# Feature chunks with 512-column matmuls, a shared last row block and folded key weights in a two-layer decoder trunk

## The chip, the cores and the metric

One NeuronCore of a Trainium2 chip runs the whole program. The metric is the device time of one execution in microseconds. A core has TensorE (PE; its weight loads are shown apart as PEld), VectorE (DVE), ScalarE (ACT), GpSimd (POOL), and SyncE (SP), whose queue issues the DMA transfers here.

## What is computed

Two layers of a decoder trunk over 256 tokens of width 2048. Cut to what matters:

```python
(r_q, r_k, r_v, a_cq, a_ckv, a_kpe, l_x, l_v, l_o, l_i, l_f, c_q, z) = _split_cols(x @ w_in, IN_SPLITS)
ret  = _merge(_head_norm(_retention(r_q, r_k, r_v, positions), ret_norm_g))
mla  = _merge(_mla(a_cq, a_ckv, a_kpe, ...))
xc   = jax.nn.silu(_causal_conv(l_x, ml_conv_w, ml_conv_b))
lq   = jnp.einsum('bshd,hde->bhse', xc_h, ml_w_q)      # 4 heads, 128x128 weights each
lk   = jnp.einsum('bshd,hde->bhse', xc_h, ml_w_k)
cell = _mlstm(lq, lk, lv, i_pre, f_pre) * jax.nn.sigmoid(l_o)
mls  = _merge(_head_norm(cell, ml_norm_g)) + ml_skip * xc
memo = _merge(_mem_attention(c_q, mem, w_mem_kv))      # 256 memory tokens
y    = jnp.concatenate([ret, mla, mls, memo], -1) * jax.nn.silu(z)
x    = _layernorm(DEEPNORM_ALPHA * x + y @ w_out, ln_g, ln_b)
```

In `_mlstm` the keys enter only through the scores of queries and keys. All data are fp32; weights are read from HBM once.

## The kernel before, in words

**Chunks and slots.** The weights of a layer are a stream of 20 chunks (`CHUNKS`): memk, memv, lx, cq, akv, aq, lv, lo, rq, rk, rv, z3, z2, z1, z0, out0 to out4. Most are 512 columns wide. Each has 16 slots, one for each block of 128 rows of its weight, so a layer has 320 slots. SP loads two slots at a time into `raw`, four pairs deep; the DMA of pair m waits until the remainder of slot 2m - 7 is done.

**High and low parts.** A product of fp32 numbers is made of three fp32r matmuls. ScalarE writes the high part of each slot (`hi`, L839), VectorE the remainder (`lo`, L1192), both in rings of five (`RING`). x (and the memory and y) are held as high and low parts too: xh, xl, mh, ml. ScalarE's hi of slot t waits until TensorE has used slot t - 5, so it runs at most five slots ahead.

**The two layouts.** In a "tok" chunk x is the weights operand and `hi` streams through: per slot 2 x (xh hi, xl hi), then 2 x (xh lo), six matmuls of 512 columns (L1125, L1126, L1129). In a "feat" chunk (memk, lx, cq, z3 to z0) the result is wanted with features on the partitions, so `hi` is the weights operand and x streams through: for four blocks j of 128 features a matmul with xh (L1135) and one with xl (L1137), 256 columns each, adding into the same half of a PSUM bank; then four with `lo` (L1141). Two accumulators of two banks are used in turn. TensorE may begin a chunk once the chunk before the last has been read.

**Other work** is put between slots by tables written out by hand: `PE_AT`, `ACT_AT`, `DVE_AT` give for a slot position the steps that an engine does after its own part of that slot, in order. Each engine has one queue, so a step that waits holds up all that stands behind it. TensorE's small products go through four more PSUM banks in turn. Those that matter here:
- memk and cq are split into high and low parts: ScalarE at 20, 22 and 68, 69, VectorE's remainders (L1277) at 21, 23 and 69, 70. `mem_scores` (L866 to L868) of head 0 stands on TensorE after slot 69 and waits for all of them. memv's copies and remainders are VectorE's at 36, 38.
- lx is copied (L696), run through a convolution on VectorE (positions 54 to 61), then silu on ScalarE at 65, 66. `ml_q` and `ml_k` (L922, fp32 matmuls, 256 columns, two instructions each) stand at 88 to 91, their copies on ScalarE at 93 to 95, the scores L964 and L965 from 110.
- x is split (`x_hi`, `x_lo`), with one x block of two per two slots, VectorE at 16 to 30 in layer 0 and at 21 to 35 in layer 1.
- `silu` of z reads the accumulator, `gate` multiplies, then y is split (`y_hi`, `y_lo`) before the out chunks.

**The end.** The last chunk of layer 1 stays resident, and TensorE does all 16 slots for rows 0 to 127 first, then for rows 128 to 255 (L1157 to L1161). VectorE does `residual(3)`, then for each row block of 128: last residual, statistics, X - mean times gain (L1618), GpSimd's power, times 1/std plus bias (L1624). Block 0 is done in 1024 columns, block 1 in 512; each piece is then stored by SP (L587). The code of VectorE's last part:

```python
for n in range(0, D_MODEL + ahead * w, w):
    if n < D_MODEL:
        blk = X[:, i, n:n + w]
        link(dve.scalar_tensor_tensor(blk, blk, ln_mv[:, i, 0:1], gb[:, 0, n:n + w],
                                      ALU.subtract, ALU.mult))
    if n >= ahead * w:
        ...
        dve.wait_ge(ln_pow.sem, ln_pow.at(l, i))
        dve.scalar_tensor_tensor(blk, blk, ln_rstd[:, i:i + 1], gb[:, 1, at], ALU.mult, ALU.add)\
           .then_inc(finished.sem, 1)
```

`link` makes VectorE wait for its own operation.

## Time and profile before

| | |
|---|---|
| median of 3 runs | 935.68 us (935.43 to 936.45) |
| profiled execution, its own time | 935.72 us |
| its span, first to last instruction | 933.9 us |
| TensorE busy | 919.6 us (98%) |
| VectorE busy | 631.9 us (68%) |
| ScalarE busy | 492.2 us (53%) |
| granted TensorE clock, mean | 0.995 |
| HBM | 184 GB/s over the span |

### The profile page before, as it was taken

To read this page: it belongs to the slowest core of one execution; us is meant where nothing else is said; L and a number is where in the kernel's file an instruction comes from. 1 tells how busy PE (TensorE), PEld (TensorE's weight loads), DVE (VectorE), ACT (ScalarE), POOL (GpSimd) and SP (SyncE) were. 2 spreads that over 40 slices of the span, in tenths; PEclk is the share of its full clock that TensorE was granted. 3 is DMA by queue.
4 is the path that set the end of the run, shared out by engine and by line. 5 is a ranking of instruction groups with operands and counts; after the bars stand their busy time and mean duration, and the time that the engine had idled before them with its cause. 6 is when DMAs were issued, how large, how long until landed. Compare 5 with 4: busy or idle time off the path is not lost.

```text
span 933.9 us, 15656 instructions
## 1 busy us (share of the span) xinstructions
PE 919.6 (98%) x5876; PEld 836.5 (90%) x5876; DVE 631.9 (68%) x1264; ACT 492.2 (53%) x925; POOL 16.0 (2%) x18
## 2 busy tenths in 40 slices
PE   8999999999999999999999999999999999999994
PEld 7899998888889999888998999888888999998894
DVE  6867677766754765665759577767577557767657
ACT  5654765544554444544576456745354544555441
POOL 0000000000000000000000000000000000000001
PEclk9999999999999999999999999999999999999998
DMA  9874546655444555663765765466355554565843
GB/s 345 307 275 161 158 137 201 212 166 178 138 159 158 169 171 180 186 195 115 249 195 191 253 210 173 142 202 180 114 156 148 171 159 151 180 186 175 289 135 126
DMA packets 51868, 172.67 MB, mean 185 GB/s; under 512 B 6216, under 2 KB 6352, under 8 KB 51152
## 3 DMA queue, kind: packets, MB, share of 16 engines
q1 hardware_dynamic: 51792, 171.66, 57.5%
q8 instruction: 47, 0.77, 0.3%
q14 instruction: 29, 0.24, 0.1%
HBM read 169.53 MB, written 2.11 MB: 184 GB/s over the span
## 4 chain that ended last, share of the span: by engine, by line
PE 95%; DVE 2%; DMA 2%; issue 0%; ACT 0%; SPq 0%; DVEq 0%; ACTq 0%
PE acc L1125 17%; PE acc L1129 17%; PE acc L1126 17%; PE acc L1135 11%; PE acc L1141 11%; PE acc L1137 11%; PE work L861 2%; DMA raw<-in_w 2%; PE work L1004 1%; PE work L922 1%; PE work L964 1%; PE work L866 1%; PE work L867 1%; PE work L868 1%; DVE X L1618 1%; PE work L1039 1%
## 5 line engine op out<-in xcount | busy, mean ns | idle before, releaser
L1192 DVE TENSOR_TENSOR lo<-raw,hi 128x512 fp32r<-128x512 f32 (+2 forms) x624 | 394.5, 646 | 278.5 <-ACT hi L839 270.9
L839 ACT ACTIVATE hi<-raw 128x512 fp32r<-128x512 f32 (+2 forms) x624 | 365.4, 595 | 348.3 <-PE acc L1129 175.2
L1125 PE MATMUL acc<-hi,xh 128*128 128x512 f32 (+2 forms) x592 | 219.3, 375 | 0.0
L1126 PE MATMUL acc<-hi,xl 128*128 128x512 f32 (+2 forms) x592 | 211.3, 362 | 0.0
L1135 PE MATMUL acc<-xh,hi 128*128 128x256 f32 x768 | 194.1, 285 | 0.0
L1137 PE MATMUL acc<-xl,hi 128*128 128x256 f32 x768 | 192.4, 283 | 0.0
L1129 PE MATMUL acc<-lo,xh 128*128 128x512 f32 (+2 forms) x592 | 166.1, 362 | 0.0
L1137 PEld LDWEIGHTS acc<-xl,hi 128*128 128x128 f32 x768 | 146.9, 191 | 0.2
L1135 PEld LDWEIGHTS acc<-xh,hi 128*128 128x128 f32 x768 | 146.8, 191 | 0.2
L1126 PEld LDWEIGHTS acc<-hi,xl 128*128 128x128 f32 x592 | 111.7, 189 | 15.0
L1125 PEld LDWEIGHTS acc<-hi,xh 128*128 128x128 f32 x592 | 111.6, 188 | 15.0
L1141 PE MATMUL acc<-xh,lo 128*128 128x256 f32 x768 | 123.4, 283 | 0.0
L1129 PEld LDWEIGHTS acc<-lo,xh 128*128 128x128 f32 x592 | 106.3, 188 | 17.1
L1141 PEld LDWEIGHTS acc<-xh,lo 128*128 128x128 f32 x768 | 105.9, 191 | 0.0
L1135 PE MATMUL acc<-mh,hi 128*128 128x256 f32 x128 | 33.0, 290 | 0.3 <-ACT hi L839 0.3
L1137 PE MATMUL acc<-ml,hi 128*128 128x256 f32 x128 | 32.6, 286 | 0.0
L1135 PEld LDWEIGHTS acc<-mh,hi 128*128 128x128 f32 x128 | 24.8, 194 | 1.5 <-issue 1.5
L1125 PE MATMUL acc<-hi,mh 128*128 128x512 f32 x64 | 25.8, 402 | 0.0
L1126 PE MATMUL acc<-hi,ml 128*128 128x512 f32 x64 | 25.0, 391 | 0.0
L1137 PEld LDWEIGHTS acc<-ml,hi 128*128 128x128 f32 x128 | 24.8, 194 | 0.1
L1141 PE MATMUL acc<-mh,lo 128*128 128x256 f32 x128 | 20.6, 283 | 0.0
L1129 PE MATMUL acc<-lo,mh 128*128 128x512 f32 x64 | 19.8, 390 | 0.0
(294 smaller groups left out, 1024.6 us busy)
## 6 DMA issues: line engine op xcount, KB each, us to landing
raw<-in_w SPq DMA_DIRECT2D x255, 512.0 KB, 3.7
raw<-in_w SPq DMA_DIRECT2D x50, 256.0 KB, 2.7
raw<-in_w SPq DMA_DIRECT2D x16, 328.0 KB, 3.2
Y<-in_wuq SPq DMA_DIRECT2D x2, 1152.0 KB, 7.8
Y<-in_x_t SPq DMA_DIRECT2D x4, 512.0 KB, 8.5
X<-in_x SPq DMA_DIRECT2D x4, 512.0 KB, 4.6
gb<-in_gb SPq DMA_DIRECT2D x1, 2048.0 KB, 7.3
Y<-in_gb SPq DMA_DIRECT2D x1, 2048.0 KB, 10.3
```

The lines of the kernel that those rows point to most:

```text
L839: act.activation(place(l, t, hi), raw[:, s, (t % 2) * w:(t % 2 + 1) * w], ACT.Copy)\
L861: return pe.transpose(dst, src, ident[0:src.shape[0], 0:src.shape[0]])
L866: pe.matmul(o, ah, bh, start=start, stop=False)
L867: pe.matmul(o, al, bh, start=False, stop=False)
L868: return pe.matmul(o, ah, bl, start=False, stop=stop)
L1125: pe.matmul(o, ah[:, kk, q], hi[:, s, 0:w], start=k == 0, stop=False)
L1126: pe.matmul(o, al[:, kk, q], hi[:, s, 0:w], start=False, stop=False)
L1129: m = pe.matmul(acc[:, p, i, 0:w], ah[:, kk, i * P:(i + 1) * P], lo[:, s, 0:w], start=False, stop=k == KT - 1)
L1135: pe.matmul(o, hi[:, s, q], ah[:, kk, :], start=k == 0 and j % 2 == 0, stop=False, skip_group_check=True)
L1137: pe.matmul(o, hi[:, s, q], al[:, kk, :], start=False, stop=False, skip_group_check=True)
L1141: m = pe.matmul(o, lo[:, s, q], ah[:, kk, :], start=False, stop=k == KT - 1, skip_group_check=True)
L1192: dve.tensor_tensor(place(*at, lo), raw[:, s, (t % 2) * w:(t % 2 + 1) * w], place(*at, hi).bitcast(F32), ALU.subtract).then_inc(lo_done.se ...
```

## The change

Three edits are made together.

1. Feature chunks are cut in halves of 256 features (`_halves`), each of 8 slots; a slot then holds two blocks of 128 rows, side by side. xh and xl lie interleaved in one buffer `xx` (mh and ml in `mm`), so that one matmul of 512 columns multiplies a block of `hi` by both; high sums lie in columns 0 to 255 of a bank and low sums in 256 to 511. ScalarE copies the low sums to SBUF (`part`), VectorE adds the high sums (`joined`) and gives the accumulator back. silu, and the splits of memk and cq, then read SBUF. memv comes ahead of memk. The number of slots stays at 320; silu, gate and split positions move.
2. In the matrix memory, Wq and Wk of a head are multiplied once (`ml_fold`, four fp32 matmuls of 128 columns, after slot 64; ScalarE's copy at 67), `ml_q` multiplies xc by that product, and the scores take xc itself as keys. `ml_k` and its copies go; `skip`, which overwrites xc, moves from 101 to 126.
3. In the last row block, VectorE does the four subtractions in a row without waiting for itself, and the final step of two of the four pieces only. For the other two TensorE adds the bias (identity times bias) and diag(1/std) times the piece in PSUM, and ScalarE copies the result. `residual(3)` of layer 1 moves from behind the stream into it, at slots 314 and 317.

```diff
-CHUNKS = [("memk", W, "feat"), ("memv", W, "tok"), ("lx", W, "feat"), ("cq", W, "feat"),
+FEAT = W // 2
+
+
+def _halves(*names):
+    return [(f"{n}{q}", FEAT, "feat") for n in names for q in range(2)]
+
+
+CHUNKS = [("memv", W, "tok"), *_halves("memk", "lx", "cq"),
           ("akv", AKV_W, "tok"), ("aq", QRANK - QHEAD, "tok"), ("lv", W, "tok"), ("lo", W, "tok"),
-          ("rq", W, "tok"), ("rk", W, "tok"), ("rv", W, "tok"),
-          ("z3", W, "feat"), ("z2", W, "feat"), ("z1", W, "feat"), ("z0", W, "feat"),
+          ("rq", W, "tok"), ("rk", W, "tok"), ("rv", W, "tok"), *_halves("z3_", "z2_", "z1_", "z0_"),
...
+SPAN = [KT // 2 if layout == "feat" else KT for _, _, layout in CHUNKS]
+WIDTH = [2 * w if layout == "feat" else w for _, w, layout in CHUNKS]
+SLOT_AT = np.concatenate([[0], np.cumsum(SPAN)]).tolist()
+PLACE = [(c, k) for c in range(NCH) for k in range(SPAN[c])]
...
-        (88, "ml_q", 0), (88, "ml_q", 1), (89, "ml_k", 0), (91, "ml_k", 1),
+        (64, "ml_fold", 0), (88, "ml_q", 0), (89, "ml_q", 1),
...
-        (20, "memk", 0), (22, "memk", 1), (52, "lx", 0), (53, "lx", 1),
-        (65, "silu_conv", 0), (66, "silu_conv", 1), (68, "cq", 0), (69, "cq", 1), (84, "akv", 0), (85, "akv", 1),
-        (93, "ml_q", 0), (94, "ml_q", 1), (95, "ml_k", 0), (95, "ml_k", 1),
+        (28, "part", "memk", 0), (36, "part", "memk", 1), (44, "part", "lx", 0), (52, "part", "lx", 1),
+        (60, "part", "cq", 0), (68, "part", "cq", 1),
+        (188, "part", "z3_", 0), (196, "part", "z3_", 1), (204, "part", "z2_", 0), (212, "part", "z2_", 1),
+        (220, "part", "z1_", 0), (228, "part", "z1_", 1), (236, "part", "z0_", 0), (244, "part", "z0_", 1),
+        (30, "memk", 0), (38, "memk", 1),
+        (65, "silu_conv", 0), (66, "silu_conv", 1), (62, "cq", 0), (70, "cq", 1), (84, "akv", 0), (85, "akv", 1),
+        (67, "ml_fold", 0), (93, "ml_q", 0), (94, "ml_q", 1),
...
-        (36, "memv", 0), (38, "memv", 1), (99, "mem_out", 0), (110, "mem_out", 1),
+        (20, "memv", 0), (22, "memv", 1),
+        (29, "joined", "memk", 0), (37, "joined", "memk", 1), (45, "joined", "lx", 0), (53, "joined", "lx", 1),
+        (61, "joined", "cq", 0), (69, "joined", "cq", 1),
+        (189, "joined", "z3_", 0), (197, "joined", "z3_", 1), (205, "joined", "z2_", 0), (213, "joined", "z2_", 1),
+        (221, "joined", "z1_", 0), (229, "joined", "z1_", 1), (237, "joined", "z0_", 0), (245, "joined", "z0_", 1),
+        (99, "mem_out", 0), (110, "mem_out", 1),
         (123, "lo", "wukv", 0), (125, "lo", "wukv", 1), (128, "lo", "ckvT", 0),
-        (21, "lo", "memk", 0), (23, "lo", "memk", 1), (69, "lo", "cq", 0), (70, "lo", "cq", 1),
+        (31, "lo", "memk", 0), (39, "lo", "memk", 1), (63, "lo", "cq", 0), (71, "lo", "cq", 1),
...
-        _put(DVE_AT, (OUT0 + _c + 1) * KT + 4, "residual", _c)
+        _put(DVE_AT, SLOT_AT[OUT0 + _c + 1] + 4, "residual", _c)
     else:
-        _put(FIRST_DVE, (OUT0 + _c + 1) * KT + 4, "residual", _c)
+        _put(FIRST_DVE, SLOT_AT[OUT0 + _c + 1] + 4, "residual", _c)
+        _put(LATER_DVE, SLOT_AT[OUT0 + _c + 1] + 4 + 6, "residual", _c, 0)
+        _put(LATER_DVE, SLOT_AT[OUT0 + _c + 1] + 4 + 9, "residual", _c, 1)
...
+        xx = sb("xx", [P, KT, 2, SEQ], F32R)
+        xh, xl = xx[:, :, 0, :], xx[:, :, 1, :]
...
+        qk = B[3][:, 0:512].rearrange("p (h d) -> p h d", h=HEADS)
...
+                if i == 0:
+                    sp.wait_ge(finished.sem, b + 1)
+                elif b < 2 + BY_MATMUL:
+                    sp.wait_ge(copied.sem, b - 2 + 1)
+                else:
+                    sp.wait_ge(finished.sem, b - BY_MATMUL + 1)
...
+                def part_(name, q):
+
+                    c = CI[f"{name}{q}"]
+                    wait_chunk(act, l, c)
+                    if (name, q) == ("z3_", 0):
+                        wait_read(act, l, ("ml_scores", 3))
+                    if (name, q) == ("z2_", 0):
+                        wait_job(act, l, ("rkT", 1))
+                    if (name, q) == ("z0_", 0):
+                        wait_job(act, l, ("retT", 1))
+                    act.activation(sums(name, q), acc[:, acc_turn(l, c)[1], :, SEQ:2 * SEQ], ACT.Copy)\
+                       .then_inc(lo_part.sem, 1)
...
+                def ml_fold(_):
+                    wait_job(act, l, ("ml_fold", 0))
+                    act.wait_ge(conv_done.sem, conv_done.at(l, 0))
+                    act.activation(qk[:, :, :], bank(l, ("ml_fold", 0)).rearrange("p (h d) -> p h d", h=HEADS), ACT.Copy)\
+                       .then_inc(free_bank(l, "ml_fold", 0), 1)
...
+                    wait_joined(act, l, f"z{g}_", i)
+                    act.activation(sums(f"z{g}_", i), sums(f"z{g}_", i), ACT.Silu).then_inc(silu_done.sem, 1)
...
+            l = DEPTH - 1
+            act.wait_ge(ln_pow.sem, ln_pow.at(l, 1))
+            act.activation(tmp[:, 0:P], ident, ACT.Copy, scale=ln_rstd[:, 1:2]).then_inc(diag_done.sem, 1)
+            for b in range(BY_MATMUL):
+                act.wait_ge(scaled.sem, b + 1)
+                act.activation(X[:, 1, b * 512:(b + 1) * 512], A_out3(b), ACT.Copy).then_inc(copied.sem, 1)
...
-                        wait_acc_read(pe, l, CI["memk"])
-                        wait_acc_read(pe, l, CI["cq"])
+                        pe.wait_ge(kq_split.sem, kq_split.at(l, 3))
...
+                def ml_fold(_):
+
+                    pe.wait_ge(lw_in.sem, lw_in.at(l, 0))
+                    o = take("ml_fold", 0)
+                    for h in range(HEADS):
+                        m = pe.matmul(o[:, h * HD:(h + 1) * HD], lw[:, 0, h, :], lw[:, 1, h, :], start=True, stop=True)
+                    m.then_inc(job_done.sem, 1)
...
+                def ml_q(q):
+                    if q == 0:
+                        wait_read(pe, l, ("ml_fold", 0))
+                    pe.wait_ge(xc_done.sem, xc_done.at(l, q))
+                    o = take("ml_q", q)
+                    for h in (2 * q, 2 * q + 1):
+                        m = pe.matmul(o[:, (h % 2) * 256:(h % 2 + 1) * 256], qk[:, h, :], xcT[:, h, :],
+                                      start=True, stop=True)
...
-                    causal_scores(take("ml_scores", h), lkT, lqT, h).then_inc(job_done.sem, 1)
+                        wait_read(pe, l, ("ml_q", 0), ("ml_q", 1))
+                    causal_scores(take("ml_scores", h), xcT, lqT, h).then_inc(job_done.sem, 1)
...
-                        for j in range(4):
-                            o, q = acc[:, p, j // 2, (j % 2) * 256:(j % 2 + 1) * 256], slice(j * P, (j + 1) * P)
-                            pe.matmul(o, hi[:, s, q], ah[:, kk, :], start=k == 0 and j % 2 == 0, stop=False,
-                                      skip_group_check=True)
-                            pe.matmul(o, hi[:, s, q], al[:, kk, :], start=False, stop=False, skip_group_check=True)
+                        for kk in range(2):
+                            x = both_parts[:, 2 * k + kk, :, :].rearrange("p a t -> p (a t)")
+                            for j in range(2):
+                                q = slice(kk * FEAT + j * P, kk * FEAT + (j + 1) * P)
+                                pe.matmul(acc[:, p, j, :], hi[:, s, q], x, start=k == 0 and kk == 0, stop=False,
+                                          skip_group_check=True)
                         pe.wait_ge(lo_done.sem, lo_done.at(l, t))
-                        for j in range(4):
-                            o, q = acc[:, p, j // 2, (j % 2) * 256:(j % 2 + 1) * 256], slice(j * P, (j + 1) * P)
-                            m = pe.matmul(o, lo[:, s, q], ah[:, kk, :], start=False, stop=k == KT - 1,
-                                          skip_group_check=True)
+                        for kk in range(2):
+                            for j in range(2):
+                                q = slice(kk * FEAT + j * P, kk * FEAT + (j + 1) * P)
+                                m = pe.matmul(acc[:, p, j, 0:SEQ], lo[:, s, q], both_parts[:, 2 * k + kk, 0, :], start=False,
+                                              stop=2 * k + kk == KT - 1, skip_group_check=True)
...
+            wait_acc_read(pe, l, LAST - 1)
+            pe.wait_ge(gb_in.sem, 16)
+            for b in range(BY_MATMUL):
+                pe.matmul(A_out3(b), ident, gb[:, 1, b * 512:(b + 1) * 512], start=True, stop=False)
+            pe.wait_ge(diag_done.sem, 1)
+            for b in range(BY_MATMUL):
+                pe.wait_ge(gained.sem, b + 1)
+                pe.matmul(A_out3(b), tmp[:, 0:P], X[:, 1, b * 512:(b + 1) * 512], start=False, stop=True)\
+                  .then_inc(scaled.sem, 1)
...
+                def joined_(name, q):
+
+                    p = acc_turn(l, CI[f"{name}{q}"])[1]
+                    dve.wait_ge(lo_part.sem, lo_part.at(l, JOINED.index((name, q))))
+                    dve.tensor_tensor(sums(name, q), acc[:, p, :, 0:SEQ], sums(name, q), ALU.add).then_inc(joined.sem, 1)
+                    wait_joined(dve, l, name, q)
+                    dve.sem_inc(acc_read[p].sem, 2)
...
-            link(residual(c - 1))
...
-                ahead = 2 * 512 // w
-                for n in range(0, D_MODEL + ahead * w, w):
-                    if n < D_MODEL:
-                        blk = X[:, i, n:n + w]
-                        link(dve.scalar_tensor_tensor(blk, blk, ln_mv[:, i, 0:1], gb[:, 0, n:n + w],
-                                                      ALU.subtract, ALU.mult))
-                    if n >= ahead * w:
-                        at = slice(n - ahead * w, n - ahead * w + w)
-                        blk = X[:, i, at]
-                        dve.wait_ge(ln_pow.sem, ln_pow.at(l, i))
-                        dve.scalar_tensor_tensor(blk, blk, ln_rstd[:, i:i + 1], gb[:, 1, at], ALU.mult, ALU.add)\
-                           .then_inc(finished.sem, 1)
+                for n in range(0, D_MODEL, w):
+                    blk = X[:, i, n:n + w]
+                    m = dve.scalar_tensor_tensor(blk, blk, ln_mv[:, i, 0:1], gb[:, 0, n:n + w], ALU.subtract, ALU.mult)
+                    m.then_inc(gained.sem, 1) if i else link(m)
+                if i:
+                    dve.wait_ge(gained.sem, D_MODEL // w)
+                dve.wait_ge(ln_pow.sem, ln_pow.at(l, i))
+                for n in range(BY_MATMUL * w if i else 0, D_MODEL, w):
+                    blk = X[:, i, n:n + w]
+                    dve.scalar_tensor_tensor(blk, blk, ln_rstd[:, i:i + 1], gb[:, 1, n:n + w], ALU.mult, ALU.add)\
+                       .then_inc(finished.sem, 1)
...
-        "lw": np.stack([np.stack([g["ml_w_q"][l], g["ml_w_k"][l]]).transpose(2, 0, 1, 3).reshape(-1) for l in range(DEPTH)]),
+        "lw": np.stack([np.stack([g["ml_w_q"][l], g["ml_w_k"][l]]).transpose(3, 0, 1, 2).reshape(-1) for l in range(DEPTH)]),
```

The rest of the diff follows from these: names and indices of accumulators, buffers for the sums, the order of the weights in HBM.

## Rows read from the trace of the kernel before

**Rows 1.** The page's part 1: busy us (share of the span), instructions.
```profile
PE 919.6 (98%) x5876; PEld 836.5 (90%) x5876; DVE 631.9 (68%) x1264; ACT 492.2 (53%) x925; POOL 16.0 (2%) x18
```

**Rows 2.** Who waited: engine, line waited for, us in total, times, longest.
```profile
ACT hi L839 <- PE acc L1129: 175.2, 261, 2.6
ACT hi L839 <- PE acc L1141: 155.2, 195, 2.2
...
PE acc L1135 <- ACT hi L839: 0.3, 1, 0.3
```

**Rows 3.** Timeline of TensorE in cq: start us, duration us, engine, line.
```profile
89.03 0.28 PE L1135 MATMUL acc<-xh,hi 128*128 128x256 f32 x1
...
90.47 0.28 PE L1135 MATMUL acc<-xh,hi 128*128 128x256 f32 x1
```

**Rows 4.** Timeline of TensorE in a token chunk, lv.
```profile
140.27 0.39 PE L1125 MATMUL acc<-hi,xh 128*128 128x512 f32 x1
...
141.63 0.39 PE L1125 MATMUL acc<-hi,xh 128*128 128x512 f32 x1
```

**Rows 5.** Timeline of TensorE in out0 of layer 1.
```profile
836.09 0.39 PE L1125 MATMUL acc<-hi,B2r 128*128 128x512 f32 x1
...
837.49 0.39 PE L1125 MATMUL acc<-hi,B3r 128*128 128x512 f32 x1
```

**Rows 6.** Groups by form: busy us, mean ns, idle before.
```profile
L1192 DVE TENSOR_TENSOR lo<-raw,hi 128x512 fp32r<-128x512 f32 x512 | 347.5, 690 | 239.9 <-ACT hi L839 232.8 <-PE acc L1129 3.2
...
L839 ACT ACTIVATE hi<-raw 128x512 fp32r<-128x512 f32 x512 | 318.6, 630 | 316.8 <-PE acc L1129 153.3 <-PE acc L1141 149.7 <-DMA raw<-in_w 12.7
...
L696 ACT ACTIVATE B<-acc 128x512 f32<-128x512 f32 x4 | 2.3, 582 | 0.0
```

**Rows 7.** Busy us of PE, PEld, DVE, ACT, POOL in two stretches of layer 1.
```profile
497.00:510.00 13.00, 13.00 (x67) 10.71 (x66) 12.53 (x23) 8.89 (x17) 0.00 (x0) 1.00 0.61 199
510.00:523.00 13.00, 13.00 (x107) 12.87 (x106) 9.89 (x16) 6.19 (x11) 0.00 (x0) 1.00 0.64 205
```

**Rows 8.** The chain in order of time, one piece.
```profile
121.10 1.73 PE work L922 x8
```

**Rows 9.** Timelines of the three engines around mem_scores(0), layer 0.
```profile
97.93 0.42 ACT L839 ACTIVATE hi<-raw 128x256 fp32r<-128x256 f32 x1 [0.33 <-PE acc L1141]
98.25 0.58 ACT L691 ACTIVATE B2r<-acc 128x512 fp32r<-128x512 f32 x1
98.73 0.41 ACT L839 ACTIVATE hi<-raw 128x256 fp32r<-128x256 f32 x1
...
99.51 0.69 DVE L1277 TENSOR_TENSOR B5r<-acc,B2r 128x512 fp32r<-128x512 f32 x1
100.11 0.42 DVE L1192 TENSOR_TENSOR lo<-raw,hi 128x256 fp32r<-128x256 f32 x1
100.45 0.69 DVE L1277 TENSOR_TENSOR B5r<-acc,B2r 128x512 fp32r<-128x512 f32 x1
...
97.67 0.28 PE L1125 MATMUL acc<-hi,xh 128*128 128x256 f32 x1
...
101.99 0.29 PE L866 MATMUL work<-B0r,B2r 128*128 128x256 f32 x1
```

**Rows 10.** Timelines of the tail, three engines.
```profile
915.31 0.39 PE L1157 MATMUL acc<-ml,xh 128*128 128x256 f32 x1
...
925.35 2.32 DVE L1618 SCALAR_TENSOR_TENSOR X<-X,ln_mv,Y 128x512 f32<-128x512 f32 x3
...
929.15 2.08 DVE L1624 SCALAR_TENSOR_TENSOR X<-X,ln_rstd,Y 128x512 f32<-128x512 f32 x3
...
925.51 0.99 POOL L597 TENSOR_TENSOR ln_rstd<-ln_stats,half 128x1 f32<-128x1 f32 x1 [4.99 <-DVE ln_stats L1612]
```

**Rows 11.** Busy time, granted clock (PEclk), DMA share, GB/s at the end.
```profile
922.00:923.00 1.00, 0.15 (x2) 0.00 (x0) 1.00 (x2) 0.00 (x0) 0.00 (x0) 1.00 0.00 0
925.00:926.00 1.00, 0.00 (x0) 0.00 (x0) 0.90 (x3) 0.00 (x0) 0.49 (x1) 0.59 0.99 406
```

224 lines of the change are left out of this document (113 added, 111 removed).

## The prediction

> **What bounds the kernel now.** I read the page's engine row first: TensorE is busy 98% of 933.9 us [rows 1]. The list of who waited for whom then says that TensorE hardly waits (0.3 us for weights once the work has begun), while ScalarE stands 175.2 + 155.2 us waiting for TensorE to give ring buffers back [rows 2]. So TensorE's queue sets the time from about 5 us to 922 us and whatever is taken from it is gained, as long as ScalarE and VectorE keep their lead, which is the ring's five slots. Behind 922 us a tail on VectorE and the stores decides (part 5). So three things are to be costed: the matmul rate of feature chunks, places where a shorter lead or a new dependency stops TensorE, and the tail.
>
> **Part 1, merged matmuls.** Two feature slots start 90.47 - 89.03 = 1.44 us apart; with 12 matmuls of 256 columns that is 0.12 us each [rows 3]. Two token slots start 141.63 - 140.27 = 1.36 us apart, 0.2267 us for each of six matmuls of 512 columns [rows 4]. The 256 columns between them take 0.1067 us, which is 2.4 GHz; the other 0.0133 us comes once for each matmul, whatever its width. The change streams the same columns in 4 matmuls of 512 and 4 of 256: 4 x 0.2267 + 4 x 0.12 = 1.387 us, 0.053 us less. Seven chunks of 16 slots in two layers are 224 slots: 11.9 us.
>
> No row has a 512-column matmul with hi as its weights. The nearest other one, with B buffers as weights in out0, takes 837.49 - 836.09 = 1.40 us for six, a fixed part of 0.020 us [rows 5]: 224 x 4 x 0.0067 = 6 us less gain. I allow as much below. I take 0.0133, which these weights (hi) and this moving operand (xh) show now.
>
> The Trainium skill (TensorE: Matmul & The Clock Gate, section Back-to-back issue gap) gives a warm start-to-start of N/2.4 + 2.5 ns, 109 and 216 ns, which speaks against this part: by it 896 vanished matmuls save 2.2 us only. This trace disagrees (120 and 227 ns).
>
> **Its price.** High and low sums now stand side by side, so each of 14 half chunks per layer costs ScalarE a copy (128x512 from PSUM, 0.58 us) and VectorE an addition (0.69 us) [rows 6]. That is 28 x 0.69 = 19 us and 28 x 0.58 = 16 us, the latter less lx's four copies. In a feature slot of 1.387 us the stream itself takes 0.63 and 0.69 us [rows 6], so both are covered by about 0.7 us of idle per slot. An accumulator is needed back 8 slots after its half chunk ends and is added up at the fifth or sixth position after it, by engines that run up to five slots ahead: no wait. Cost 0; with the lead gone, each addition would cost up to 0.69 us.
>
> The lead is thinnest where x is split. In layer 1 from 497 to 510 us VectorE is busy 12.53 of 13.00 us, and 9.89 in the next 13 [rows 7]. There the change puts memv's four operations (2.7 us, in place of memk's two, 1.3) and, by position 39, two additions and memk's two remainders (2.6 us): 4 us more, against a lead that I estimate at 4 to 5 us (five slots of 1.44 less the stream's own 1.3 and what the split takes). I take 0; bounds 0 and 2 us per layer.
>
> **Part 2, folded key weights.** Eight instructions of L922 (256 columns; an fp32 matmul is two instructions) run in 1.73 us, 0.216 each, and each layer has 16 [rows 8]. The change leaves 8 and adds a fold of four matmuls of 128 columns, 8 instructions. I estimate those at half of 0.216: 0.87 us. Saved 2 x (1.73 - 0.87) = 1.7 us; bounds 1.3 (fixed parts as in part 1) and 2.0.
>
> **Part 3, where the fold and the halves land.** The fold stands after slot 64, ScalarE's copy of it at position 67. ScalarE reaches 67 while TensorE is at slot 63, so it stops there, in order, until the fold is through. Behind it are queued hi(68), the part copy of cq1, hi(69), hi(70), the high part of cq1 and hi(71); VectorE's addition (69) and remainder (71) of cq1 wait for them, and TensorE wants that last remainder for mem_scores(0) after slot 69. Before, the second cq remainder (B5r) ran 100.45 to 101.14 and mem_scores started at 101.99: a margin of 0.85 us [rows 9].
>
> With time 0 at the start of slot 64 (97.67 before) and the spacings of rows 9 (hi 0.32, copy 0.48, lo 0.34, remainder 0.60, next slot's start to the reader 0.26):
> - the fold ends at 0.72 + 0.87 = 1.59, its copy starts at 1.85;
> - hi(68) 2.33, part 2.65, hi(69) 3.13 to 3.55;
> - VectorE lo(69) 3.59, addition 3.93 to 4.62;
> - high part of cq1 4.67, hi(71) 5.17 to 5.59;
> - lo(71) 5.62, remainder of cq1 5.96 to 6.65; TensorE may go at 6.7.
>
> TensorE is there at 1.59 + 5 x 0.72 = 5.19. So it stands 1.5 us in each layer: +3.0 us. Bounds 0 (the margin swallows it) and 2.5 us each.
>
> **Part 4, the start.** memv comes first, a token chunk of 1.36 instead of 1.44 us per slot. The first two slots lie ahead of TensorE's only wait for weights, so 2 x 0.08 us is not gained: +0.2.
>
> **Part 5, the tail.** Of row block 1 VectorE now does four subtractions and two final operations, TensorE two blocks. VectorE's last eight operations run from 925.35 to 931.23 [rows 10]. After: start 925.5 (below), six at 0.69 with no wait between the four, done 929.7, 1.5 us earlier. TensorE: the power takes 0.99 us [rows 10], so it is ready at 926.65; diagonal by ScalarE, about 0.3, 927.0; product 4 x 0.216 = 0.86, copy 0.58: block 0 at 928.8, block 1 at 929.6. But four stores leave through SP in the order b2, b3, b4, b5. Now 2.67 us lie between VectorE's last operation and the end; 262 KB at 406 GB/s [rows 11] are 0.65 us of that, and I put 1.0 ahead of the flow and 1.0 behind it. One after another: b3 flows from 930.6, b4, b5 until 932.6, the end 933.65 instead of 933.9: -0.25 us. Most of what VectorE saves goes to the stores. Bounds -1.5 and +1.
>
> Moving residual(3) into slots 314 and 317 frees VectorE earlier, but puts 0.8 us twice between remainders for which TensorE already waits (a start is late at 915.31 [rows 10]). TensorE's first half ends 0.9 us later, VectorE starts block 0 0.1 us later; that is in the numbers above.
>
> **Sum** against the profiled execution's own 935.72 (span 933.9 and 1.8 around it; the median of the runs, 935.68, is the same within 0.04): 935.7 - 11.9 - 1.7 + 3.0 + 0.2 - 0.25 = **925.1 us**.
>
> **Rivals.**
> - *The keys' wait does not come*, the margin of rows 9 absorbs it: 922.1. For it: TensorE never waits now. Against: the order of the positions. Chance 0.14.
> - *The clock falls before the products.* It fell at about 925.2, 3.0 us after the last matmul [rows 11]. Now TensorE works on the bias blocks until 924.8 and resumes at 927.1, a gap of 2.3 us. If it falls, two products take 1.72 us each, b3 is ready at 931.3, SP holds b4 and b5 behind it, the end is near 934.8: 926.3. Chance 0.16.
> - *VectorE's lead runs out while x is split*: 1 to 4 us, 927.5. Chance 0.12.
> - *A merged matmul costs 0.233* as in rows 5: 931.1. Chance 0.04.
> - *A merge saves hardly anything*, 2.2 us in place of 11.9 (what the page cited above would give): 934.8, no change. Rows 3 and 4 speak against it. Chance 0.04.
> - *Slower: accumulators come back late.* With each half chunk's addition exposed (28 x 0.69), 925.1 + 19 = 944. It decides from 10.6 / 28 = 0.38 us per half chunk. Against it: 0.7 us of idle per slot. Chance 0.03.
>
> My forecast has 0.47. The range 921 to 929 holds it and the first three rivals, 0.89 together, less their edges. About 0.2% (1.9 us) is what a measurement of this kernel can tell from no change. Faster by more: 0.93; within it 0.04; slower by more 0.03.
>
> **What would show it.** Part 1: a z slot starts every 1.387 us. Part 2: 8 fold instructions in 0.87 us after slot 64. Part 3: TensorE idle for about 1.5 us ahead of mem_scores(0) in each layer, released by VectorE's remainder of cq. Part 5: granted clock 1.0 in the products, stores back to back. The prediction is wrong if z slots stay at 1.44, if TensorE has no such gap, or if waits for lo appear between slots 20 and 40.

## The result and the profile after

The changed kernel takes **929.53 us** (median of 4 runs, 929.0 to 929.95), the kernel before 935.96 beside it. The ratio is 0.9928, 95% interval 0.9916 to 0.9940: faster by 6.4 us where 10.6 were forecast, and 0.5 us above the range. The profiled execution took 929.15 us, its span is 927.4 us.

The page's part 1 of the kernel after, answering to [rows 1]:

```profile
PE 912.3 (98%) x4988; PEld 788.5 (85%) x4988; DVE 646.6 (70%) x1290; ACT 502.9 (54%) x950; POOL 16.0 (2%) x18
```

TensorE has 888 matmuls fewer, and VectorE and ScalarE are 14.7 and 10.7 us busier, as the change says. The list of who waited for whom (us in total, times, longest), answering to [rows 2]:

```profile
ACT hi L906 <- PE acc L1212: 162.3, 222, 2.6
...
ACT hi L906 <- PE acc L1226: 131.2, 192, 2.1
...
PE work L941 <- DVE B5r L1371: 2.7, 2, 1.4
PE acc L1257 <- ACT tmp L914: 2.3, 1, 2.3
...
PE acc L1208 <- ACT hi L906: 1.8, 1, 1.8
PE acc L1247 <- DVE mm L1288: 0.9, 2, 0.5
```

ScalarE still waits for ring buffers, 293 us where it was 330, so TensorE still sets the time. TensorE's new waits are the keys' (L941, two times), the one for the diagonal in the tail (L1257), a longer one at the start (L1208; 0.3 before), and two for remainders in the first half of the last tile (L1247), where `residual(3)` now stands between them. There is none for lo while x is split.

**Feature slots.** Timeline of TensorE in cq of layer 0, answering to [rows 3] (start, duration, engine, line; x4 is four matmuls in a row):

```profile
89.75 1.09 PE L1220 MATMUL acc<-xx,hi 128*128 128x512 f32 x4
90.68 0.63 PE L1226 MATMUL acc<-xx,lo 128*128 128x256 f32 x4
91.15 1.09 PE L1220 MATMUL acc<-xx,hi 128*128 128x512 f32 x4
92.08 0.64 PE L1226 MATMUL acc<-xx,lo 128*128 128x256 f32 x4
92.56 1.09 PE L1220 MATMUL acc<-xx,hi 128*128 128x512 f32 x4
...
93.96 1.09 PE L1220 MATMUL acc<-xx,hi 128*128 128x512 f32 x4
```

Three slots take 93.96 - 89.75 = 4.21 us, 1.403 each, not 1.387. The four wide matmuls (512 columns) take 0.93 us instead of 4 x 0.2267 = 0.91; the four narrow ones (256 columns) 0.47 to 0.48, as they should.

**The keys.** Timelines of the three engines from slot 64 to `mem_scores(0)` in layer 0, answering to [rows 9]:

```profile
97.48 1.05 PE L994 MATMUL work<-B 128*128 128x128 f32 x8
98.29 0.36 PE L1208 MATMUL acc<-hi,xx 128*128 128x256 f32 x1
...
98.57 0.60 ACT L831 ACTIVATE B<-work 128x512 f32<-128x512 f32 x1 [1.70 <-PE work L994]
...
99.37 0.59 ACT L767 ACTIVATE B<-acc 128x512 f32<-128x512 f32 x1
...
101.35 0.63 ACT L754 ACTIVATE B2r<-B 128x512 fp32r<-128x512 f32 x1 [0.79 <-DVE B L1647]
...
100.64 0.68 DVE L1647 TENSOR_TENSOR B<-acc,B 128x512 f32<-128x512 f32 x1
...
102.67 0.68 DVE L1371 TENSOR_TENSOR B5r<-B,B2r 128x512 fp32r<-128x512 f32 x1
...
103.50 0.35 PE L941 MATMUL work<-B0r,B2r 128*128 128x256 f32 x1 [1.37 <-DVE B5r L1371]
```

One link after the other: ScalarE stood 1.70 us for the fold, the part copy (L767) came after it, then VectorE's addition (L1647), the high part (L754), the remainder (L1371), and TensorE, idle for 1.37 us.

**The tail.** Timelines of TensorE, VectorE and ScalarE at the end of the kernel after, answering to [rows 10]:

```profile
916.34 1.88 PE L1253 MATMUL acc<-Y,ident 128*128 128x512 f32 x4
920.48 1.98 PE L1257 MATMUL acc<-X,tmp 128*128 128x512 f32 x4 [2.26 <-ACT tmp L914]
...
917.42 0.42 DVE L1708 SCALAR_TENSOR_TENSOR X<-X,acc 128x256 f32<-128x256 f32 x1
...
918.84 2.73 DVE L1717 SCALAR_TENSOR_TENSOR X<-X,ln_mv,Y 128x512 f32<-128x512 f32 x4
921.60 1.42 DVE L1724 SCALAR_TENSOR_TENSOR X<-X,ln_rstd,Y 128x512 f32<-128x512 f32 x2
...
922.50 0.60 ACT L917 ACTIVATE X<-acc 128x512 f32<-128x512 f32 x1 [0.26 <-PE acc L1257]
```

The products (L1257, four instructions) ran at the full clock, 1.98 us in all. VectorE does the four subtractions in a row (L1717) and two final operations (L1724). It ends at 923.0, ScalarE at 923.1, yet the program goes on to 927.4. The same stretch in windows (busy time of PE, PEld, DVE, ACT, POOL, then granted clock, DMA share, GB/s):

```profile
923.00:924.00 1.00, 0.00 (x0) 0.00 (x0) 0.01 (x1) 0.10 (x1) 0.00 (x0) 1.00 0.75 277
924.00:925.00 1.00, 0.00 (x0) 0.00 (x0) 0.00 (x0) 0.00 (x0) 0.00 (x0) 1.00 1.01 373
925.00:926.00 1.00, 0.00 (x0) 0.00 (x0) 0.00 (x0) 0.00 (x0) 0.00 (x0) 1.00 1.05 354
```

With no engine at work, the last four blocks (1.05 MB) drain until a little past 926.

### The profile page after: what moved, and what is told of

It reads as the page before. It is cut to its first block, busy times and chain, and to the rows that moved or that the text cites. A ratio compares the mean times of both kernels' runs of the same rounds, so it can differ in the third digit from the quotient of the medians.

```text
span 927.4 us, 13974 instructions
## 1 busy us (share of the span) xinstructions
PE 912.3 (98%) x4988; PEld 788.5 (85%) x4988; DVE 646.6 (70%) x1290; ACT 502.9 (54%) x950; POOL 16.0 (2%) x18
## 4 chain that ended last, share of the span: by engine, by line
PE 95%; DMA 1%; DVE 1%; issue 1%; ACT 1%; POOL 0%; SPq 0%; POOLq 0%; DVEq 0%
PE acc L1220 22%; PE acc L1208 17%; PE acc L1212 17%; PE acc L1209 17%; PE acc L1226 11%; PE work L936 2%; DMA raw<-in_w 1%; PE work L1084 1%; PE work L1044 1%; PE work L941 1%; PE work L942 1%; PE work L943 1%; PE work L1119 1%; PE work L1120 1%; PE work L1069 1%
## 5 line engine op out<-in xcount | busy, mean ns | idle before, releaser
L1208 PE MATMUL acc<-hi,xx 128*128 128x512 f32 (+2 forms) x592 | 219.4, 375 | 0.0
L1209 PE MATMUL acc<-hi,xx 128*128 128x512 f32 (+2 forms) x592 | 211.2, 361 | 0.0
L1220 PE MATMUL acc<-xx,hi 128*128 128x512 f32 x768 | 211.1, 396 | 0.0
L1212 PE MATMUL acc<-lo,xx 128*128 128x512 f32 (+2 forms) x592 | 166.1, 362 | 0.0
L1220 PEld LDWEIGHTS acc<-xx,hi 128*128 128x128 f32 x768 | 131.3, 189 | 17.6
L1226 PEld LDWEIGHTS acc<-xx,lo 128*128 128x128 f32 x768 | 117.7, 189 | 16.4
L1209 PEld LDWEIGHTS acc<-hi,xx 128*128 128x128 f32 x592 | 111.7, 189 | 14.9
L1208 PEld LDWEIGHTS acc<-hi,xx 128*128 128x128 f32 x592 | 111.6, 188 | 14.9
L1226 PE MATMUL acc<-xx,lo 128*128 128x256 f32 x768 | 122.0, 281 | 0.0
L1212 PEld LDWEIGHTS acc<-lo,xx 128*128 128x128 f32 x592 | 106.2, 188 | 16.9
L1220 PE MATMUL acc<-mm,hi 128*128 128x512 f32 x128 | 35.5, 399 | 0.0
L1208 PE MATMUL acc<-hi,mm 128*128 128x512 f32 x64 | 25.5, 399 | 1.8 <-ACT hi L906 1.8
L1209 PE MATMUL acc<-hi,mm 128*128 128x512 f32 x64 | 24.9, 389 | 0.0
L1208 PEld LDWEIGHTS acc<-hi,mm 128*128 128x128 f32 x64 | 12.1, 189 | 5.3 <-DVE mm L1293 2.2
```

Of the source, the lines that this page charges most:

```text
L1208: pe.matmul(o, ah[:, q], hi[:, s, 0:w], start=k == 0, stop=False)
L1209: pe.matmul(o, al[:, q], hi[:, s, 0:w], start=False, stop=False)
L1212: m = pe.matmul(acc[:, p, i, 0:w], ah[:, i * P:(i + 1) * P], lo[:, s, 0:w], start=False, stop=k == KT - 1)
L1220: pe.matmul(acc[:, p, j, :], hi[:, s, q], x, start=k == 0 and kk == 0, stop=False, skip_group_check=True)
L1226: m = pe.matmul(acc[:, p, j, 0:SEQ], lo[:, s, q], both_parts[:, 2 * k + kk, 0, :], start=False, stop=2 * k + kk == KT - 1, skip_group_chec ...
```

## The experiments

Differences are against the changed kernel unless another is named; times are medians of several executions, but of a single one for the kernels of "Layout, order, place", "All eight matmuls wide" and "Ring slots shifted". Of diffs the deciding lines are shown; "..." marks what is left out. The kernel before ran beside each batch (935.8 to 936.3).

### Where the merge's gain went

**The merge alone undone.** hi meets the high and the low x in two matmuls into the same bank.

```diff
-    pe.matmul(acc[:, p, j, :], hi[:, s, q], x, ...)
+    pe.matmul(acc[:, p, j, 0:SEQ], hi[:, s, q], x[:, 0:SEQ], ...)
+    pe.matmul(acc[:, p, j, SEQ:2 * SEQ], hi[:, s, q], x[:, SEQ:2 * SEQ], ...)
```

> The changed kernel with the merge alone undone: in a feature chunk hi still meets the high and the low x, but in two matmuls of 256 columns into the two halves of the same accumulator, 12 matmuls a slot. Order, layout, additions, fold and tail stay. Theory: each matmul costs 0.12 us as before, a slot 1.44 us, so 224 slots take 224 x (1.44 - 1.4035) = 8.2 us more than the changed kernel: 937.7, which is slower than the kernel before by the additions' side effects, the keys' wait and the tail. Rival (a merge saves only 2.5 ns for each matmul that is gone, and the shorter slot has another cause such as the layout of x): slot near 1.41 us, 2.2 us more: 931.7.

937.88 us; every feature slot without other work takes 1.44. Timeline of TensorE in cq:

```profile
89.79 0.28 PE L1220 MATMUL acc<-xx,hi 128*128 128x256 f32 x1
...
91.23 0.28 PE L1220 MATMUL acc<-xx,hi 128*128 128x256 f32 x1
```

91.23 - 89.79 = 1.44 us, 0.12 for each of twelve. So the merge is worth 937.88 - 929.53 = 8.35 us, 0.037 us per slot, and the other parts together cost 1.7 us against the kernel before that ran beside it (936.19; ratio 1.0017, 1.0008 to 1.0027). The ten executions of this kernel lie between 936.3 and 938.8, so TensorE's own way says it more firmly. Its first matmul of the last tile, in the kernel before, the changed one and this one:

```profile
909.59 0.28 PE L1157 MATMUL acc<-ml,B1r 128*128 128x256 f32 x1
902.73 0.28 PE L1243 MATMUL acc<-mm,B1r 128*128 128x256 f32 x1
911.02 0.28 PE L1245 MATMUL acc<-mm,B1r 128*128 128x256 f32 x1
```

911.02 - 902.73 = 8.3 us is the merge, 911.02 - 909.59 = 1.4 us all the rest ahead of the last tile.

**Layout, order, place.** Three kernels ask what makes a merged matmul dearer than the 0.2267 us of a token slot. In the first, high and low x are in separate halves of the buffer:

```diff
-        xx = sb("xx", [P, KT, 2, SEQ], F32R)
+        xx = sb("xx", [P, 2, KT, SEQ], F32R)
...
```

> The changed kernel with the high and the low x in two separate halves of their buffer, so that a merged matmul of 512 columns reads two runs of 256 columns 2,048 elements or more apart instead of one run of 512. Theory A (the larger fixed part, 0.233 us for each merged matmul, comes from something else, such as which buffer holds the weights): feature slots stay at 1.40 us, 929 in all. Theory B (it comes from how the moving operand is laid out): feature slots move by more than 0.01 us, to 1.387 if this layout is the better one (925.5) or above 1.41 if it is worse (over 931).

929.25 us, slots unchanged: 1.403. (Here the granted clock fell within the products at the end, 0.73 from 920 to 921 us and 0.50 behind, which made the tail 1.0 us longer; more on this under "The tail".) Next, the two loops exchanged:

```diff
-    for kk in range(2):
-        x = both_parts[:, 2 * k + kk, :, :]...
-        for j in range(2):
+    for j in range(2):
+        for kk in range(2):
+            x = both_parts[:, 2 * k + kk, :, :]...
```

> The changed kernel with the loops of a feature slot exchanged: both inner pieces (kk) of one half (j) behind each other, so that the accumulator buffers of two matmuls that follow each other are 0,0,1,1 as in token slots, and the moving operand changes with each matmul. Theory (a merged matmul's 0.233 us comes from changing the accumulator bank, or from two matmuls with one moving operand): slot 1.36 to 1.39 us, 2 to 9 us less than the changed kernel's 929.5. Rival (it comes from the weights' side): slot stays at 1.40, time at 929.5.

928.75 us, slots 1.403. And the rings placed first in SBUF:

```diff
+        hi, lo = sb("hi", [P, RING, 512], F32R), sb("lo", [P, RING, 512], F32R)
         X = sb("X", [P, NT, D_MODEL])
...
-        hi, lo = sb("hi", [P, RING, 512], F32R), sb("lo", [P, RING, 512], F32R)
```

> The changed kernel with the rings of hi and lo weights placed in front of all other buffers of SBUF instead of behind them; no instruction changes otherwise. Theory: the fixed part of a matmul depends on where the weights lie beside the moving operand (512 columns take 0.227 us where a ring buffer moves and xx is the weights, 0.233 where a later buffer is the weights); then the feature slots fall to 1.36 to 1.387 us and the token slots may rise from 1.36 to 1.40 us. With 224 feature slots and 400 token slots: anywhere from 926 to 941. Rival (the place in SBUF plays no part): 1.40 and 1.36 us stay, 929.5 in all.

928.36 us, feature slots 1.403, token slots 1.36. Of each of the three there is one execution, 0.3 to 1.2 us below the changed kernel's median, and feature slots have no part in that: in the traces the mean distance from one matmul of a feature slot to the next moved by less than 1 ns at each of its eight places. Neither the moving operand's layout nor the order of banks nor which buffer lies first is the cause.

**All eight matmuls wide.**

```diff
-    m = pe.matmul(acc[:, p, j, 0:SEQ], lo[:, s, q], both_parts[:, 2 * k + kk, 0, :], ...)
+    m = pe.matmul(acc[:, p, j, :], lo[:, s, q], <both halves, 512 columns>, ...)
```

> The changed kernel with lo too meeting the high and the low x in one matmul of 512 columns: it adds the product of the two low parts, which neither kernel computes, so a feature slot has eight matmuls of 512 columns and no narrow one. What sets the time of a merged matmul? Theory A (the mixture of 512 and 256 columns within a slot costs it): all eight take 0.2267 us, slot 1.813 us. Theory B (hi or lo as weights with x moving cost 0.233 whatever stands beside them): slot 1.87 us. 224 slots longer by 0.41 or 0.46 us: 1,021 or 1,033 us in all; the slot is what counts here.

1,022.77 us. Timeline of TensorE in cq:

```profile
99.83 1.07 PE L1220 MATMUL acc<-xx,hi 128*128 128x512 f32 x4
...
103.45 1.07 PE L1220 MATMUL acc<-xx,hi 128*128 128x512 f32 x4
```

(103.45 - 99.83) / 16 = 0.226 us per matmul, with the same hi, x, banks and places. Theory A holds: a merged matmul costs what a token matmul costs as long as no narrow one stands in the slot.

**Feature slots in pairs.** The wide matmuls of two slots, then the narrow ones of both; the base also has the fold moved and the B buffers placed alike (both below).

```diff
+    for u in () if k % 2 == 0 else (t - 1, t):
+        pe.wait_ge(lo_done.sem, lo_done.at(l, u))
+        ... the four lo matmuls of slot u ...
```

> The kernel with all B buffers placed alike (expected at 924.8), and feature slots taken in pairs: the hi matmuls of two slots (eight of 512 columns), then the lo matmuls of both (eight of 256). Same matmuls, half as many changes of width. A pair takes 2.807 us now; 2.773 is what it would be with 227 and 120 ns each. Theory A (each change of width costs, or disturbs the matmuls for a while): the pair falls by half of the difference or more, 0.017 to 0.034 us x 112 pairs = 1.9 to 3.8 us less: 921.0 to 922.9. Theory B (narrow and wide matmuls in one slot cost the same however they are ordered): pair stays at 2.80, 924.8. Rival on the other side: ring buffers come free one slot later, ScalarE's lead of 4.7 us shrinks and TensorE starts to wait for hi or lo: over 925.

924.89 us. Timeline of TensorE: the first pair of memk, which comes behind a token chunk, then a pair of cq:

```profile
29.45 1.98 PE L1221 MATMUL acc<-mm,hi 128*128 128x512 f32 x8
31.26 1.12 PE L1229 MATMUL acc<-mm,lo 128*128 128x256 f32 x8
...
90.88 2.00 PE L1221 MATMUL acc<-xx,hi 128*128 128x512 f32 x8
92.72 1.11 PE L1229 MATMUL acc<-xx,lo 128*128 128x256 f32 x8
93.67 1.09 PE L1221 MATMUL acc<-xx,hi 128*128 128x512 f32 x4
```

Behind wide matmuls, eight wide ones take 31.26 - 29.45 = 1.81 us, 0.2267 each. Behind narrow ones the same eight take 92.72 - 90.88 = 1.84 us. Going from narrow to wide costs about 0.03 us, and a pair has one such change: 2.79 us where two slots took 2.81. In the trace the five wide matmuls behind a change start 0.228 to 0.236 us apart, the next ones 0.227.

The mechanism is theory A's, the size is not. A pair fell by 0.014 us and not by 0.017 or more: the change is felt over five wide matmuls, a slot has only four of them and is 0.016 us dearer than 1.387, a pair has all five and is 0.020 dearer than 2.773. And the time missed theory A's 921.0 to 922.9. It is 0.3 us below its base, but TensorE reached the last tile at 898.90 us and in the base at 898.42; that it is no slower comes from the tail, where the base's clock fell in the profiled execution and this one's did not (below). The wait for cq grew (1.2 us in all instead of 0.5).

### Where the weights lie

**Ring slots shifted.** The rings' rows are made 520 elements long.

```diff
-        hi, lo = sb("hi", [P, RING, 512], F32R), sb("lo", [P, RING, 512], F32R)
+        hi, lo = sb("hi", [P, RING, 520], F32R), sb("lo", [P, RING, 520], F32R)
```

> The changed kernel with ring slots 2,080 instead of 2,048 bytes apart, so that each of the five slots starts at another offset (0, 32, 64, 96 and 128 bytes); the buffers allocated behind the rings move by 320 bytes. Theory: if the fixed part depends on how the addresses of weights and moving operand stand to each other, slot times spread with a period of five slots, by 0.01 us or more. Rival: address plays no part; every feature slot stays at 1.40 to 1.406, the first 8 slots of out0 at 1.40 and the others at 1.36; 929.5 in all.

934.30 us, 4.8 more. The slots of cq repeat with a period of five, 1.415, 1.405, 1.401, 1.416, 1.396 us, where they were 1.401 and 1.406 in turn: the theory's spread. Timeline of TensorE in the second half of out0, where xx holds the weights:

```profile
387.24 0.39 PE L1208 MATMUL acc<-hi,xx 128*128 128x512 f32 x1
...
388.64 0.39 PE L1208 MATMUL acc<-hi,xx 128*128 128x512 f32 x1
...
390.01 0.40 PE L1208 MATMUL acc<-hi,xx 128*128 128x512 f32 x1
...
391.40 0.39 PE L1208 MATMUL acc<-hi,xx 128*128 128x512 f32 x1
```

1.40, 1.37 and 1.39 us where all were 1.36. So the place of an operand does count, in steps much finer than which buffer comes first.

**B buffers at multiples of 128 bytes.** From here to the end of this section the base is the kernel with the fold moved (next section, 926.41). X, xx, mm, hi and lo all start 128 bytes past a multiple of 2,048; B1 to B3 start 1,984 past one and B0 1,952. The edit moves these four.

```diff
+        sb("gap", [P, 24])
...
-            size = {0: NT * HEADS * (HD + 1), 3: 4 * (SEQ + PAD)}.get(i, 4 * SEQ)
+            size = {0: NT * HEADS * (HD + 1) + 24, 3: 4 * (SEQ + PAD) + 16}.get(i, 4 * SEQ)
```

> The kernel with the fold moved behind the keys (926.4), and with gaps of 96, 96 and 64 bytes in SBUF so that the B buffers start at multiples of 128 bytes, as xx, mm and the rings do. Before, B1 to B3 start 64 bytes and B0 32 bytes off such a multiple; they hold the weights of the first 8 slots of each out chunk. Theory (a 512-column matmul takes 0.233 instead of 0.227 us where an operand isn't aligned to 128 bytes, as the shifted ring made token slots slower): these slots fall from 1.40 to 1.36 us, 0.71 to 0.68 in the half-wide ones; 6 x 8 x 0.04 = 1.9 us less, and 0.4 to 1 for out3 and out4: 923.8 to 924.5. Rival (alignment isn't what slows them): 1.40 stays, 926.4.

925.31 us, 1.1 less than its base. Timeline of TensorE in out0 of layer 1 (weights B1, B2, B3, then B0):

```profile
823.91 0.39 PE L1209 MATMUL acc<-hi,B1r 128*128 128x512 f32 x1
...
825.27 0.39 PE L1209 MATMUL acc<-hi,B2r 128*128 128x512 f32 x1
...
832.11 0.40 PE L1209 MATMUL acc<-hi,B0r 128*128 128x512 f32 x1
...
833.51 0.40 PE L1209 MATMUL acc<-hi,xx 128*128 128x512 f32 x1
```

825.27 - 823.91 = 1.36 us with B1, 833.51 - 832.11 = 1.40 with B0, which now stood at a multiple of 2,048, 128 bytes off the others. The theory was half right: two of eight slots stayed slow, and the time missed its 923.8 to 924.5. The 256-wide slots of out3 and out4 got slower, from 0.71 to 0.72, which takes back 0.2 us.

**All placed alike.**

```diff
+        stats, rstd = sb("stats", [P, 8, 6]), sb("rstd", [P, 8])      # moved here, fills 224 bytes
         B, Br = [], []
...
-            size = {0: NT * HEADS * (HD + 1), 3: 4 * (SEQ + PAD)}.get(i, 4 * SEQ)
+            size = {0: NT * HEADS * (HD + 1) + 56, 3: 4 * (SEQ + PAD) + 20}.get(i, 4 * SEQ)
```

> The kernel with the fold moved behind the keys (926.4), with B0 to B3 all placed at 128 bytes past a multiple of 256, as xx, mm and the rings are (buffers of statistics and gaps fill the space). With B0 at a multiple of 256 and B1 to B3 as here, only six of the first eight slots of an out chunk had fallen to 1.36 us (925.3); those with B0 stayed at 1.40. Theory (what counts is that weights and moving operand stand alike to a multiple of 256 bytes): all eight take 1.36, six chunks x 2 x 0.04 = 0.5 us less than with six: 924.8. Rival (B0's slots are slow for another reason): 1.40 stays there, 925.3.

925.20 us. All eight early slots take 1.36 us, now with B0 too (timeline of out0 in layer 1):

```profile
829.79 0.39 PE L1209 MATMUL acc<-hi,B0r 128*128 128x512 f32 x1
...
831.15 0.39 PE L1209 MATMUL acc<-hi,B0r 128*128 128x512 f32 x1
```

With weights and moving operand alike to 256 bytes every wide matmul behind wide ones takes 0.2267 us, and where they are not, up to 0.236. The fixed 0.020 us of [rows 5] was this and had nothing to do with hi or x. TensorE reached the last tile 1.2 us earlier than in the kernel with six fast slots (0.3 of it from the start), and yet the time is the same; the tail took it back (below).

### The keys' wait

```diff
-        (64, "ml_fold", 0), ...      # TensorE
+        (76, "ml_fold", 0), ...
-        (67, "ml_fold", 0), ...      # ScalarE's copy
+        (82, "ml_fold", 0), ...
```

> The changed kernel with the fold moved from slot 64 to slot 76 and ScalarE's copy of it from position 67 to 82, nothing else. Theory: TensorE's wait for the remainder of cq in front of the first memory scores (slot 69; the slot with it takes 3.04 us against 1.43, 1.6 us in each layer) comes from ScalarE standing for the fold with the pieces of cq behind it. With the copy behind them the wait shrinks to what the late high part of cq1 alone gives, 0.3 us a layer or less: 2.6 us less than the changed kernel, near 926.9. Rival: the wait comes from the addition and the two remainders of cq themselves, which are new or later in VectorE's order; then it stays at 1.3 to 1.6 us a layer and the time at 929.5.

926.41 us, 3.1 less (ratio to before 0.990, 0.9885 to 0.9915). The waits of TensorE in this kernel:

```profile
PE acc L1208 <- ACT hi L906: 0.5, 1, 0.5
PE work L941 <- DVE B5r L1371: 0.5, 2, 0.2
```

2.7 us of waiting became 0.5. The fold's place made the wait; the new additions leave 0.2 us per layer. The 3.1 us are not all the keys', though. In the traces the stretch from slot 64 to slot 82 is 1.15 us shorter in each layer, 2.3 in all; 0.3 us lie at the start and 0.6 between the start of the last tile and VectorE's first operation on row block 1, where no fold stands.

### The tail

All on the kernel with the fold moved (926.4). **The residual put back** behind the stream:

```diff
-        _put(LATER_DVE, SLOT_AT[OUT0 + _c + 1] + 4 + 6, "residual", _c, 0)
-        _put(LATER_DVE, SLOT_AT[OUT0 + _c + 1] + 4 + 9, "residual", _c, 1)
...
+            link(residual(c - 1))
             dve.wait_ge(gb_in.sem, 16)
```

> The kernel with the fold moved behind the keys (926.4), and the last residual addition but one of layer 1 put back to where it was before the change, behind the remainders, ahead of the last tile. Theory: at 0.8 us twice it delayed the remainders for which TensorE already waits; back in its old place TensorE ends its first half 0.5 to 0.9 us earlier and VectorE starts row block 0 0.1 to 0.4 us earlier after the start of the last chunk (7.8 instead of 8.24 us): 926.0 to 926.3. Rival: VectorE is what decides there; with 1.7 us of work put back in front of row block 0 it starts no earlier, and the time stays or rises by up to 0.3: 926.4 to 926.7.

927.72 us, 1.3 more, which neither theory gave. Timeline of TensorE and a window of that kernel:

```profile
912.43 1.88 PE L1251 MATMUL acc<-Y,ident 128*128 128x512 f32 x4
917.38 3.64 PE L1255 MATMUL acc<-X,tmp 128*128 128x512 f32 x4 [3.07 <-ACT tmp L912]
...
917.00:918.00 1.00, 0.62 (x1) 0.50 (x2) 1.00 (x3) 0.33 (x1) 0.00 (x0) 0.66 0.00 0
```

Counted from the start of the last tile, TensorE finished 0.4 us earlier and VectorE came 0.4 us later than with the fold moved, so TensorE stood 3.07 us instead of 2.27; the granted clock fell (0.66 in this microsecond, 0.50 or 1.2 GHz behind it) and the products took 3.64 us instead of 1.98. This is the rival "the clock falls before the products", in a kernel one edit away.

**No block on TensorE.**

```diff
-BY_MATMUL = 2
+BY_MATMUL = 0
```

> The kernel with the fold moved behind the keys (926.4), with no block of the last tile on TensorE: VectorE does all four subtractions and all four final operations of row block 1, as in the kernel before. Theory: VectorE ends 1.5 us later, but its last stores then leave one by one instead of in a bunch behind a full queue; the time is 926.2 to 926.8, so that sharing the end with TensorE is worth nothing within 0.3 us. Rival: the shared end saves VectorE's whole 1.5 us, and taking it back costs as much: 927.9.

926.14 us, the same within 0.3 as with two blocks on TensorE, as its theory said.

**The same with the B buffers placed alike,** without and with pairs:

> The kernel with all B buffers placed alike (925.2), with no block of the last tile on TensorE: VectorE does all of row block 1. Theory (in that kernel the granted clock fell while TensorE waited for the diagonal, so that its second product took 1.67 instead of 0.86 us and the last stores left late): without products the end comes 24.2 us after the start of the last chunk instead of 25.1, so 924.3 or less. Rival (the stores or VectorE are what decides, not the products): 925.2 or, since VectorE then works 1.5 us longer, up to 926.7.

> The kernel with all B buffers placed alike and feature slots in pairs (924.9), with no block of the last tile on TensorE. Theory: a pair of slots keeps its 2.793 us, 112 x 0.013 = 1.5 us less than in the kernel of e13_aligned_vector; the wait for cq that pairs lengthened (1.2 us in all instead of 0.5) takes 0.7 of it back: 0.8 us less than e13_aligned_vector, near 923.5. Rival: the end decides alone and pairs bring nothing: the same time as e13_aligned_vector within 0.3.

924.53 us (ratio to before 0.9875, 0.986 to 0.989), 0.7 less than with two blocks on TensorE, and 924.56. The kernel with two blocks on TensorE and these buffers had this timeline of TensorE and this window:

```profile
911.25 1.88 PE L1254 MATMUL acc<-Y,ident 128*128 128x512 f32 x4
915.28 3.26 PE L1258 MATMUL acc<-X,tmp 128*128 128x512 f32 x4 [2.15 <-ACT tmp L915]
...
916.00:917.00 1.00, 1.00 (x2) 0.45 (x2) 0.96 (x2) 0.13 (x1) 0.00 (x0) 0.50 0.00 0
```

Its clock fell within the products. So it did with high and low x apart and with all eight matmuls wide. Measured from VectorE's first operation on row block 1 to the end:

| kernel | products | first operation, end | us |
|---|---|---|---|
| before | none | 923.87, 933.9 | 10.0 |
| changed | full clock | 917.42, 927.4 | 10.0 |
| fold moved | full clock | 914.25, 924.2 | 9.95 |
| no block on TensorE | none | 914.50, 924.4 | 9.9 |
| placed alike, none on TensorE | none | 912.39, 922.3 | 9.9 |
| six slots fast | full clock | 913.18, 923.1 | 9.9 |
| pairs | full clock | 913.41, 923.3 | 9.9 |
| all wide | clock fell | 1010.51, 1021.0 | 10.5 |
| high and low x apart | clock fell | 916.55, 927.5 | 10.9 |
| placed alike | clock fell | 912.22, 923.4 | 11.2 |
| residual put back | clock fell | 914.32, 925.9 | 11.6 |

With the products at the full clock, sharing the end is worth nothing; with the clock down it costs 0.5 to 1.7 us. Pairs do not bring their 112 x 0.013 = 1.5 us either. Between the two kernels without blocks on TensorE the feature stretches got 0.7 us shorter by the traces, the longer wait for cq took 0.7 back, and the start was 0.3 later; the forecast of 923.5 was wrong.

## Why the prediction was wrong, point by point

- **The bound** was right: TensorE's queue sets the time until the tail, and additions and copies were hidden (no wait of TensorE for lo between slots 20 and 40).
- **Part 1, the failed step.** "I take 0.0133" as the fixed part of each matmul. A feature slot is not made of 1.387 us but of 1.403, so 224 slots gave 8.35 us by the run without the merge, not 11.9. In the profiled execution 4.1 us are missing. The last tile was to start 11.9 + 1.7 - 3.0 - 0.2 = 10.4 us earlier and started 909.59 - 902.73 = 6.9 us earlier, 3.5 us short; the other parts should have moved it 1.5 us later, and with the merge undone it was 1.4 us later. So the merge is all of the 3.5, and the rest is the tail's. The price holds for slots of one width (0.12 and 0.2267 us, measured again in two kernels); both rows that I took it from had one width only. A slot of four wide and four narrow ones pays 0.016 us more, for the change from narrow to wide. The bound from [rows 5] allowed 6 us where 3.5 were lost, but for another cause: those slots have one width, and their B weights lie otherwise to the ring than xx does. The rival "a merged matmul costs 0.233" came nearest: the wide ones took 0.93 / 4 = 0.2325 us, and only the narrow ones behind them, a little shorter, kept the slot at 1.403. It had a chance of 0.04, and [rows 5] had shown its price.
- **The page's rule** (the Trainium skill, TensorE: Matmul & The Clock Gate, section Back-to-back issue gap: N/2.4 + 2.5 ns, by which the merge saves an estimated 2.2 us) does not hold here: undoing the merge costs 8.35 us, and slots of one width take 120 and 227 ns per matmul, not 109 and 216. The section means it for the gap of an isolated matmul and says that a stream with weight loads is spaced otherwise, so it was not the rule for this case.
- **Part 2** was right: 98.29 - 97.48 = 0.81 us to the next slot's first matmul, a little more with its late start, against 0.87.
- **Part 3** was right in mechanism and size: 1.37 us of standing and a slow start behind it, 1.6 us in a layer against 1.5. The chain ran as laid out: from the start of slot 64 (96.76) the copy came at 1.81 us, the part copy at 2.61, the addition 3.88, the high part 4.59, the remainder 5.91 and TensorE at 6.74, against 1.85, 2.65, 3.93, 4.67, 5.96 and 6.7. The cause, the fold's copy ahead of cq's pieces, is shown by moving it (2.2 of 2.7 us of waiting gone).
- **Part 4**: TensorE's wait for hi was 1.8 us. In the profiled executions of the fourteen other kernels that begin with memv it was between nothing and 1.1 us (0.5 with the fold moved), so a good part of it belongs to this execution and not to the change. The slot behind the wait began at 10.3 us here, at 9.6 to 10.3 in the fourteen, and at 9.6 before; so the start cost up to 0.7 us where 0.2 was forecast. What made that up ahead of the last tile was not separated.
- **Part 5**: -0.25 was forecast, the tail was no shorter than before from VectorE's first operation on row block 1, and VectorE came there 0.4 us later after TensorE's start of the last tile (0.1 forecast for block 0). That 0.4 is within what the kernels with memv first differ by (13.5 to 15.1 us; 14.3 before, 14.7 here). That VectorE's 1.5 us would go to the stores was right: its work ends 4.4 us before the end where it was 2.7.
- **The clock** stayed up in the profiled execution, as forecast, but that was partly luck. Eleven kernels with products at the end were traced besides; in four of them the clock fell before or within the products. Two of the changed kernel's four executions have a mean granted clock of 1.000 and took 929.0 and 929.15 us; the other two, with 0.996 and 0.997, took 929.91 and 929.95, and 0.996 is also the mean of the kernel with x apart, whose clock fell within the products. That those two lost their clock there is an estimate from their means. So this rival's 0.16 looks too low.

What stays open is why a change from narrow to wide matmuls costs 0.03 us over five matmuls, and why the place of the operands modulo 256 bytes counts. The runs show both and not their mechanism.

## What to carry to other kernels

Price a mixture of instruction shapes from a row with that mixture: per-instruction costs from uniform stretches need not add up. Where a helper step is placed between others by hand, look at what stands behind its copy in that engine's order. Handing the end's work to another engine gained nothing here, where the stores end last, and handing it to TensorE made the end depend on its clock.
